# Sums over partitions of w_ada's products: from a pair of matmuls for every 256 columns to block transposes on VectorE and four joint matmul groups

## What is computed

```python
mod = (jax.nn.silu(c) @ w_ada[l] + b_ada[l]).reshape(b, N_SUB, 3, D_MODEL)
def sublayer(h, i, fn, resid_w):
    shift = mod[:, i, 0, None, :]
    scale = mod[:, i, 1, None, :]
    gate = mod[:, i, 2, None, :]
    u = rms_norm_2(h, norm_pre[l, i]) * (1.0 + scale) + shift
    return h + resid_w * gate * rms_norm_2(fn(u), norm_post[l, i])
```

## Time and profile before

| | |
|---|---|
| median of 3 runs | 1384.12 us (1381.2 to 1384.41) |
| profiled execution, its own time | 1381.89 us |
| its span, first to last instruction | 1380.2 us |
| mean granted TensorE clock | 0.996 |
| PE busy | 1333.6 us, 97% |
| DVE busy | 988.6 us, 72% |
| ACT busy | 626.8 us, 45% |
| mean DMA rate | 183 GB/s |

### The profile page before, as it was taken

The page is one execution under the profiler, slowest core; times in us unless marked ns, Lnnn a source line. Parts: engine busy times, 40 slices in busy tenths (PEclk is TensorE's granted clock), DMA queues, the critical chain, the costliest instruction groups (busy, mean ns, idle before and its releaser), DMA issues.

```text
span 1380.2 us, 28314 instructions
## 1 busy us (share of the span) xinstructions
PE 1333.6 (97%) x11355; PEld 1285.9 (93%) x11355; DVE 988.6 (72%) x1358; ACT 626.8 (45%) x714; POOL 71.5 (5%) x103
## 2 busy tenths in 40 slices
PE   7999999999999998999999999999999999999998
PEld 6998799999999888999999999999999899999986
DVE  6766678887677764788876777777887547986644
ACT  5255554344254344544443544433644564644433
POOL 3000000000001000000000011100001000000000
PEclk9999999999999999999999999999999999999999
DMA  7752165567856423555677688897466345575543
GB/s 209 213 150 65 62 214 174 176 198 198 228 170 196 125 93 122 179 179 185 185 198 216 197 272 265 263 263 225 160 228 232 101 137 161 186 235 178 187 159 122
DMA packets 243806, 252.20 MB, mean 183 GB/s; under 512 B 4809, under 2 KB 228300, under 8 KB 243732
## 3 DMA queue, kind: packets, MB, share of 16 engines
q1 hardware_dynamic: 232464, 211.96, 50.3%
q0 software_dynamic: 11072, 39.14, 8.4%
q10 hardware_dynamic: 196, 0.06, 0.0%
HBM read 250.08 MB, written 1.05 MB: 182 GB/s over the span
## 4 chain that ended last, share of the span: by engine, by line
PE 73%; DVE 12%; ACT 8%; issue 5%; DMA 2%; DVEq 0%; ACTq 0%; SPq 0%
PE ps L2218 60%; ACT w_hi L462 4%; PE ps L2840 4%; DVE w_lo L1106 4%; DVE proj L1126 1%; DMA raw<-in_ffn_w_down 1%; PE ps L2241 1%; ACT scratch L680 1%; PE ps L2185 1%; PE ps L2367 1%; PE ps L2606 1%; DVE x_lo L1294 0%; PE ps L2557 0%; PE ps L2432 0%; PE ps L2484 0%
## 5 line engine op out<-in xcount | busy, mean ns | idle before, releaser
L1106 DVE TENSOR_TENSOR w_lo<-raw,w_hi 128x2048 fp32r<-128x2048 f32 (+1 forms) x185 | 443.0, 2395 | 203.6 <-ACT w_hi L462 202.4
L2218 PE MATMUL ps<-x_hi,w_hi 128*128 128x272 f32 (+2 forms) x2016 | 582.9, 289 | 5.4 <-DVE w_lo L1106 1.6
L2218 PE MATMUL ps<-x_hi,w_lo 128*128 128x272 f32 (+2 forms) x2016 | 575.2, 285 | 0.0
L462 ACT ACTIVATE w_hi<-raw 128x2048 fp32r<-128x2048 f32 (+1 forms) x185 | 369.5, 1998 | 387.4 <-PE ps L2218 337.9
L2218 PE MATMUL ps<-x_lo,w_hi 128*128 128x272 f32 (+2 forms) x1856 | 529.9, 285 | 0.0
L2218 PEld LDWEIGHTS ps<-x_hi,w_hi 128*128 128x128 f32 x2016 | 382.0, 189 | 9.0 <-issue 3.8
L2218 PEld LDWEIGHTS ps<-x_hi,w_lo 128*128 128x128 f32 x2016 | 382.3, 190 | 0.0
L2218 PEld LDWEIGHTS ps<-x_lo,w_hi 128*128 128x128 f32 x1856 | 351.8, 190 | 0.6 <-issue 0.3
L2218 PE MATMUL ps<-g_hi,w_hi 128*128 128x256 f32 (+2 forms) x576 | 164.4, 285 | 4.4 <-DVE g_lo L1851 1.7
L2218 PE MATMUL ps<-g_hi,w_lo 128*128 128x256 f32 (+2 forms) x576 | 163.3, 283 | 0.0
L2218 PE MATMUL ps<-g_lo,w_hi 128*128 128x256 f32 (+2 forms) x576 | 162.8, 283 | 0.0
(11 more groups left out here) (380 smaller groups left out, 1606.8 us busy)
## 6 DMA issues: line engine op xcount, KB each, us to landing
raw<-in_ffn_w_gate SPq DMA_DIRECT2D x44, 1024.0 KB, 5.4
raw<-in_ffn_w_up SPq DMA_DIRECT2D x44, 1024.0 KB, 5.4
v_tok<-in_w_ada POOLq DMA_DIRECT2D x72, 512.0 KB, 4.6
raw<-in_ffn_w_down SPq DMA_DIRECT2D x24, 1408.0 KB, 7.1
raw<-in_w_in SPq DMA_DIRECT2D x20, 1024.0 KB, 5.2
raw<-in_hgrn_w_in SPq DMA_DIRECT2D x16, 1024.0 KB, 5.6
raw<-in_fox_w_in SPq DMA_DIRECT2D x15, 1024.0 KB, 5.8
raw<-in_ffn_w_down SPq DMA_DIRECT2D x11, 1024.0 KB, 4.9
```

Source lines behind the costliest of these rows:

```text
L462: nc.scalar.activation(w_hi[s][:, 0:size], raw[s][:, 0:size], ACT.Copy).then_inc(hi_ready, 1)
L1106: V.tensor_tensor(w_lo[s][:, 0:size], raw[s][:, 0:size], w_hi[s][:, 0:size].bitcast(F32), ALU.subtract).then_inc(lo_ready, 1)
L2218: ins = T_.matmul(dst, fixed, moving, start=(kt == 0 and i == 0), stop=(kt == kts - 1 and i == 2))
```

## The change

VectorE now does most of the sum over partitions. Behind the last step of each pair, `ada_half` turns the 32x32 blocks of `ada_sum` (`transpose`, into `ada_acc`) and adds up the 32 values of each block row (`tensor_reduce`), which gives eight numbers on each partition, stored in the table `ada_parts` (128 x 288). Three waits on DVE's own semaphores stand around the two new instructions. The four quarters of 32 partitions each hold a part of the sums of different columns. PE joins them with `modulation_sums(a, b)`: four matmuls with a 128x128 window of the table `strips` as weights and b - a columns of `ada_parts`, into PSUM bank 7. It is called four times: for columns 0 to 18 ahead of `hgrn_out`, 18 to 48 between `glu1_up` and `glu1_down`, 48 to 64 behind `branch`, 64 to 72 behind `glu2_up`. Each waits until DVE has stored all pairs that its columns come from (`ada_part`).

The 36 calls of `ada_sums` are gone, and with them the wait for `ada_done` in `ada_half`. The readers move: `modulation_0` from `hgrn_in` to `hgrn_out`; `modulation_post0` is folded into `modulation_1`, which now stands between `glu1_up` and `glu1_down` instead of behind `glu1_down`; `modulation_2` moves from behind `mix_in` to ahead of `mix_out`; `modulation_3` moves from ahead of the last pair of `glu2_up` to behind it. The copy of four sums in `fox_in` goes. `strips` is a new constant of 128 x 224, loaded by one more DMA on POOL's queue.

```diff
             def ada_half(p, s):
                 if s == 0:
-                    dve.wait_ge(ada_mult, p * 2 + 2)
+                    dve.wait_ge(ada_part, p + 1)
...
-                        if whole:
-                            dve.wait_ge(ada_done, p * 2 + 2)
...
                 ins.then_inc(ada_mult, 1)
+                if s == 1:
+                    dve.wait_ge(ada_mult, p * 2 + 4)
+                    V.transpose(ada_acc, ada_sum).then_inc(ada_turned, 1)
+                    dve.wait_ge(ada_turned, p + 1)
+                    V.tensor_reduce(ada_parts[:, bass.ds(p * 8, 8)], ada_acc.rearrange("p (b c) -> p b c", c=ROWS_32), AX_X, ALU.add).then_inc(ada_part, 1)
...
-            def ada_sums(p):
-                pe.wait_ge(ada_mult, p * 2 + 4)
-                for s in range(2):
-                    T_.matmul(ps[:, 5, bass.ds(p * 2 + (ADA_COL + s), 1)], ada_sum[:, s * P:(s + 1) * P], ones[:, 0:1],
-                              start=True, stop=True).then_inc(ada_done, 1)
+            parts = ada_parts[:].rearrange("p (c q) -> p q c", q=4)
+
+            def modulation_sums(a, b):
+                pe.wait_ge(const_landed, 16 * 10)
+                pe.wait_ge(ada_part, b // 2 + 1)
+                for q in range(4):
+                    at = (3 - q) * ROWS_32
+                    ins = T_.matmul(ps[:, ADA_BANK, a:b], strips[:, at:at + P], parts[:, q, a:b], start=(q == 0), stop=(q == 3))
+                ins.then_inc(ada_done, 1)
...
-                            if add and s == 1:
-                                ada_sums(it + ada_before)
...
-            gemm("hgrn_in", q_normed, k=1, before_last=modulation_0)
+            gemm("hgrn_in", q_normed, k=1)
...
-            gemm("hgrn_out", residual(2, UNUSED), defer=True, ada="hgrn_out",
+            gemm("hgrn_out", residual(2, UNUSED), defer=True, ada="hgrn_out", before_last=modulation_0,
...
                 gemm("glu1_up", evac, late=True, ada="glu1_up")
+                modulation_1()
...
+            modulation_2()
             gemm("mix_out", gained_pair, defer=True)
...
+            pool.dma_start(strips[:], dram["const_strips"]).then_inc(const_landed, 16)
+            pool.wait_ge(const_landed, 16 * 10)
...
-            gemm("glu1_up", from_tiles(4, 1), xh, xl, SEQ, ada="glu1_up", sums=(1, 11), outer=(2, None))
-            gemm("glu1_down", from_hidden(2), gh, gl, SEQ, ada="glu1_down", sums=(0, 4))
+            gemm("glu1_up", from_tiles(4, 1), xh, xl, SEQ, outer=(2, None))
+            modulation_sums(18, 48)
+            gemm("glu1_down", from_hidden(2), gh, gl, SEQ)
```

## The result

| | before | after |
|---|---|---|
| median | 1383.84 us (4 runs, 1381.2 to 1384.41) | 1395.72 us (4 runs, 1393.99 to 1398.74) |
| profiled execution, its own time | 1381.89 us | 1395.29 us |
| span | 1380.2 us | 1393.6 us |
| mean granted clock | 0.996 | 0.990 |
| ratio, 95% interval | | 1.0094 [1.0075, 1.0113] |

The change makes the kernel slower by 0.94%, 10 to 16 us of 1384. Forecast were 1392.4 (8.3 us slower) in a range of 1387.0 to 1399.0. The two profiled executions lie 13.4 us apart, and those 13.4 us are what the rest explains.

A forecast was written before the change was run, and what follows sets the result against it. PE, 97% busy, was taken as the bound overall, with DVE or ACT and DVE setting the pace in places. 7.5 us won, 5.3 lost to DVE work and 10.5 at the border gave +8.3: 1392.4 us, range 1387 to 1399.

The forecast's parts named there:

- The border: Between glu1_up and glu1_down: PE waits for p = 23's store, 8.2 us lost, 10.5 with half clock and slower group.
- The group: Columns 18 to 48 at the glu1_up to glu1_down border: PE's four joining fp32 matmuls take 0.85 us.
- The half clock: Behind PE's 10 us of idleness before glu1_down: granted clock 0.50, 2.3 us lost including the slower group.
- The new DVE work: Behind every pair: transpose and reduction at 0.42 us each plus 0.05 for semaphore waits, 0.9 us a pair.
- Rival (a): DVE turns blocks slowly, 1.4 us a pair: 14.3 us slower in all, 1398.4 us; chance 0.14.
- The sum over the unhidden places: Places where DVE's extra work meets no slack, from ffn0_up to glu2_up: 5.3 us lost in all.
- p = 12 has slack: In ffn1_down only p = 10 and 11 pay for the new DVE work, +1.8 us; p = 12 pays nothing.
- `ffn0_up` and `hgrn_in`: At p = 3 and p = 8 DVE has no idle time before its next work: +0.9 us each.
- `mix_in` (0.4): Border behind mix_in, p = 31: 0.9 us later, but 0.5 of modulation_2 goes ahead: +0.4 us.
- The rule of the Trainium skill: Calls tensor_reduce VectorE's slowest hot-path operation, advises restructuring; weighed against the 0.42 us row for 256 elements.
- The removed sums: 36 ada_sums calls gone from PE: 16 x 0.45 + 0.2, plus 0.1 for fox_in's copy, 7.5 us won.
- The count from the chain of waits: Of 36 calls 23 bind; six struck, one kept at 0.2 us, 16 worth 0.45 us each.

The follow-up runs named there:

- e1_group_split: Kernel after, with columns 18 to 26 summed between glu1_up and glu1_down and 26 to 48 behind glu1_down; 1386.73 us, ratio 1.0026 against before.
- e3_no_sum_matmuls: Kernel before, with the two matmuls left out in 34 of the 36 ada_sums calls, waits kept, output wrong; 1378.47 us, ratio 0.9964.
- e2_dve_added: Kernel before, all sums still on PE, plus each pair's block transpose and reduction on DVE, result unread; 1391.18 us, ratio 1.0058.
- e4_busy_border: Kernel after, with 36 dummy matmuls in PE's queue ahead of the group of columns 18 to 48; 1395.38 us, ratio 1.0095 against before.

## Why the prediction was right, and where it was small

**The border, forecast 10.5, measured 11.4.** The mechanism, its place and its length held: the wait is 10.04 us, released by L1137, where some 10 were forecast. Two terms of the sum were a little off. The group took 1.70 us and not 0.85, since it ran at half clock itself. The half clock cost 2.2 us behind it (5.05 us for 24 matmuls instead of 24 x 0.118), where the forecast had 2.3 for both. The splitting of the group (`e1_group_split`) brought back 10.5 us behind the wait and 9.2 of the whole border in the profile, and 9.4 by the ratios.

**The new DVE work, forecast 0.9 us a pair, measured 0.93 to 1.04.** Rival (a) is out. The sum over the unhidden places failed in two steps. "p = 12 has slack" was wrong: DVE's h L1230 of the next unit stands behind the new pair there too, ACT waits for it and the next weights with it. So `ffn1_down` pays three times, 1.13, 1.13 and 1.03 us (1.04 for the two instructions, 0.09 for a longer gap ahead of h), and 0.2 at its end: 3.5 instead of 1.8. And in `glu2_up` 0.8 us were lost where 0 was forecast. I had taken the 12.00 us of a window for the length of a pair. By the starts of w_lo the pairs of before last 11.3 to 12.0 us, and after's 12.16, with DVE busy for nearly all of it (the stretch is one pair):

```profile
1215.90:1228.00 12.10, 11.71 (x98) 11.53 (x97) 11.58 (x20) 5.38 (x5) 1.50 (x2) 1.00 0.81 264
```

`ffn0_up` and `hgrn_in` came as said, and `hgrn_out` cost 0.4 instead of 0.6. Without `mix_in` (0.4), the forecast for this part was 4.9 us, and 7.6 were measured. The rule of the Trainium skill that the prediction weighed ("VectorE: DVE Perf Modes", section "Rules for kernel authors"), with `tensor_reduce` as the slowest operation of VectorE, would have misled here: 0.420 us for the reduction is less than the 0.446 of the transpose and the 0.484 of each SCALAR_TENSOR_TENSOR beside it, all of 256 columns.

**The removed sums, forecast 7.5 us, measured 8.2.** A pair of `glu1_up` lasts 11.36 us. The near match is in part luck: some 0.6 of the 8.2 is scatter at the start (see the table), one call more, in `hgrn_in`, is counted in the row of the mixer, and one call is worth 0.40 to 0.45 us and not always 0.45. The count from the chain of waits was the right tool; `e3_no_sum_matmuls` shows 17 such steps without the rest of the change (one is given back at once), where the prediction counted 16.

**What was missing: 2.6 us around the mixer.** I had asked of each place which engine waits for which, and never looked at PE's own stops, though one of 2.35 us stood in the trace of before. And I gave half clock a price at one border alone. In after it also falls behind the wait for p = 8's w_lo:

```profile
435.41 0.29 PE L2220 MATMUL ps<-x_hi,w_lo 128*128 128x272 f32 x1
437.88 0.36 PE L2220 MATMUL ps<-x_hi,w_hi 128*128 128x272 f32 x1 [2.17 <-DVE w_lo L1110]
```

```profile
438.40:441.80 3.40, 3.40 (x17) 3.40 (x16) 2.07 (x1) 0.66 (x1) 0.00 (x0) 0.51 0.82 244
756.00:759.40 3.40, 3.40 (x18) 3.40 (x17) 0.97 (x3) 2.54 (x2) 0.75 (x1) 0.51 1.01 324
```

17 matmuls took 3.4 us where 27 would run at full clock, and the lag rises by 1.6. The fall near 756 us in `ffn1_down` costs nothing, since PE waits for DVE at the end of that unit anyway. Before's fall near 549 us, ahead of `hgrn_out`, is gone, and the lag falls by 1.3 there. It is tempting to say that the first group, 0 to 18, fills PE's wait. But `e2_dve_added` and `e3_no_sum_matmuls` have no group there, PE waits 1.36 and 1.1 us in both, and their clock stays at 1.00 as well. So these 1.3 us are a loss that of all profiles only before's has. The parts (+1.6 behind p = 8, -1.2 and -0.4 up to the stop, +3.9 at it with the fall of the clock and the second stop, -1.3) are the 2.6.

What stays open: whether the clock falls behind a given wait is not the same in each profile. The wait behind p = 3 is followed by a fall near 284 us in `e1_group_split`, `e2_dve_added` and `e4_busy_border`, for 1.5 us, and by none in after, whose code up to there is that of the first and the third. No run shows what decides it. It may be part of why the runs of one kernel lie several us apart. Terms of 1.5 us could be told from each other only in profiles, and each kernel has one profile.

## What to carry to other kernels

A matmul that joins results of another engine is cheap, but it stands in PE's queue with all the work behind it: ask which producer it waits for is the last one in time, and split the group there. 0.9 us more on an engine that is "72% busy" cost nothing at about two thirds of the 36 places and full price at most of the others, and moving the two instructions behind the next evacuation, into that engine's own wait, made them free in `ffn1_down`. Where one stage is made faster, look at what the next one loads: pairs shortened by 0.41 us each gave up to 5 us of wait and half clock at a border that the weights' landing and DVE's steps set.

## What the hardware did that I had not expected

- PE stops in the middle of its own work, by all signs for its own code. In a mixer with runs of small matmuls (122 of them in 1.4 us) the longest stop was 1.3 to 4.4 us in every kernel, at a place that 64, 128 or 192 more instructions at the program's start moved. A change that removes instructions far ahead can so cost or win 2 to 3 us, and the granted clock fell to 0.5 behind some of these stops.
- An increment of a semaphore by PE, nothing else, takes 0.15 us (24.60 less 14.83 us for 64 of them).
- A block transpose of 128x256 float32 takes DVE 0.446 us, hardly more than a reduction of the same 256 columns to 8 (0.420).
- A wait of about 2 us on PE can be enough for half clock behind it (2.17 us at 437.88, 2.07 us at 754.72 in after), and one of 3.54 us in `e1_group_split` was not followed by any.
- The landing of the same 1408 KB at the same border, in four kernels that do the same there, came up to 3 us apart (ACT's wait was 3.80 to 6.86 us).
